# Hybrid trunk on one core: a reordered opening on five PSUM banks, a reordered last head, and the causal mask added by VectorE in seven heads

## The reference

```python
s = jnp.einsum('blhd,bshd->bhls', q_blk, k_all).astype(jnp.float32) * scale
s = s + jnp.moveaxis(fq_blk, 2, 1)[..., None] - f_k[:, :, None, :]
s = jnp.where(key_pos[None, :] <= pos_blk[:, None], s, -jnp.inf)
p = jax.nn.softmax(s, axis=-1).astype(v_all.dtype)
return jnp.einsum('blhs,bshd->blhd', p, v_all)   # indices 'bhls,bshd->blhd' in the original
```

## Time and profile before

| what | value |
|---|---|
| median of 3 runs | 1576.07 us (1575.6 to 1576.43) |
| the profiled execution, its own time | 1575.49 us |
| its span, first to last instruction | 1573.8 us |
| PE busy | 1534.6 us (98%), 9472 matmuls |
| DVE / ACT / POOL busy | 794.0 / 677.1 / 444.7 us |
| granted TensorE clock, mean | 0.999 |

### The profile page before, as it was taken

The page is one execution under the profiler, slowest core; times in us unless marked ns, Lnnn a source line. Parts: engine busy times, 40 slices in busy tenths (PEclk is TensorE's granted clock), DMA queues, the critical chain, the costliest instruction groups (busy, mean ns, idle before and its releaser), DMA issues.

```text
span 1573.8 us, 26349 instructions
## 1 busy us (share of the span) xinstructions
PE 1534.6 (98%) x9472; PEld 1415.8 (90%) x9472; DVE 794.0 (50%) x1751; ACT 677.1 (43%) x1258; POOL 444.7 (28%) x268
## 2 busy tenths in 40 slices
PE   6999999999999999999999999999999999999998
PEld 5999999999999999988888898999999999988776
DVE  5546777676884231436475243444344343435432
ACT  6444443433233322335455344445454545455321
POOL 1214453553221111344343221222222231215000
PEclk9999999999999999999999999999999999999999
DMA  5122223213102111254456536614241423213121
GB/s 154 43 70 61 74 62 101 60 45 86 53 27 57 41 40 40 79 175 160 153 192 145 56 75 53 68 37 74 37 71 44 71 41 63 61 44 141 55 98 70
DMA packets 129510, 121.09 MB, mean 77 GB/s; under 512 B 10290, under 2 KB 113292, under 8 KB 129452
## 3 DMA queue, kind: packets, MB, share of 16 engines
q1 hardware_dynamic: 129452, 120.32, 31.5%
HBM read 101.64 MB, written 18.66 MB: 76 GB/s over the span
## 4 chain that ended last, share of the span: by engine, by line
PE 88%; ACT 4%; DVE 3%; issue 3%; DMA 1%; POOL 1%; SPq 0%; ACTq 0%; DVEq 0%; POOLq 0%
PE PB L759 83%; PE PB L763 5%; DMA XT<-in_x_prompt_dram 1%; ACT L1339 1%; ACT L1804 1%; ACT SB L1893 0%; ACT SQJ L1373 0%; DVE XT L1931 0%; DMA WOR<-in_w_out_odd_dram 0%; DVE SB L1928 0%; ACT WH L1333 0%; POOL WL L626 0%; DMA XS<-in_x_prompt_dram 0%; DVE XS L1928 0%; DVE M L1931 0%
## 5 line engine op out<-in xcount | busy, mean ns | idle before, releaser
L759 PE MATMUL PB<-HH,WH 128*128 128x352 f32 x1872 | 617.5, 330 | 2.5 <-DVE HL L1924 1.6
L759 PE MATMUL PB<-HH,WL 128*128 128x352 f32 x1872 | 601.9, 322 | 0.0
L759 PE MATMUL PB<-HL,WH 128*128 128x352 f32 x1872 | 601.1, 321 | 0.0
L759 PEld LDWEIGHTS PB<-HH,WH 128*128 128x128 f32 x1872 | 351.9, 188 | 17.5 <-issue 10.4
L759 PEld LDWEIGHTS PB<-HL,WH 128*128 128x128 f32 x1872 | 352.9, 189 | 0.2
L759 PEld LDWEIGHTS PB<-HH,WL 128*128 128x128 f32 x1872 | 351.9, 188 | 0.0
L626 POOL TENSOR_TENSOR WL<-WRAW,WH 128x1024 fp32r<-128x1024 f32 x81 | 199.9, 2468 | 534.3 <-ACT WH L1333 527.6
L1333 ACT ACTIVATE WH<-WRAW 128x1024 fp32r<-128x1024 f32 x112 | 118.0, 1054 | 14.3 <-DMA WRAW<-in_w_out_even_dram 6.1
L1893 ACT ACTIVATE SB<-SB,small 128x128 f32<-128x128 f32 (+8 forms) x72 | 53.8, 748 | 78.6 <-DVE small L1928 78.6
L1924 DVE TENSOR_TENSOR Y<-PB,Y 128x128 f32 (+3 forms) x72 | 20.2, 281 | 127.6 <-PE PB L759 127.5
L759 PE MATMUL PB<-PT,VTOK 128*128 128x128 f32 (+2 forms) x624 | 81.5, 274 | 0.0
(11 more groups left out here) (312 smaller groups left out, 2362.6 us busy)
## 6 DMA issues: line engine op xcount, KB each, us to landing
WRAW<-in_w_out_even_dram SPq DMA_DIRECT2D x48, 512.0 KB, 3.6
WRAW<-in_w_in_even_dram SPq DMA_DIRECT2D x44, 512.0 KB, 3.8
WRAW<-in_w_in_odd_dram SPq DMA_DIRECT2D x32, 512.0 KB, 8.2
ACSB<-acs_rows SPq DMA_DIRECT2D x16, 528.0 KB, 5.3
NFB<-nf_rows SPq DMA_DIRECT2D x8, 656.0 KB, 3.9
XS<-in_x_prompt_dram SPq DMA_DIRECT2D x8, 512.0 KB, 6.2
XT<-in_x_prompt_dram SPq DMA_DIRECT2D x8, 512.0 KB, 5.3
x_rows<-OG SPq DMA_DIRECT2D x8, 512.0 KB, 5.4
```

What stands on the lines that cost most here:

```text
L759: return pe.matmul(out, lhsT, rhs, start=start, stop=stop)
```

## The change

- Opening. SP issues the parameter loads after x tile 1, not after tile 2. ACT loads the root's table by a dummy Sqrt before any data is there, and then works tile by tile (square, root). PE turns each of the first three tiles as soon as it is normed, five column blocks into banks 3 to 7, and the parameter rows into bank 2 after tile 0; DEXP is turned later. The first weight tile's chunk 0 is run without turns between, and the turns of group 1 are interleaved with the second weight tile.
- Mask. In heads 0 to 6 the mask matmul is left out; DVE adds `MASKD` to the diagonal 128 columns (PSUM to `SB`), and then runs the bias-and-maximum instruction on them from `SB` to `SB`. The last head keeps the matmul on PE, with one more memset on DVE.
- Last head. `fill` takes a new group bank by bank; ACT's `out_squares` stand ahead of `probs_read`; `YH` of head 6 is copied after the third output weight's high part; POOL's `out_low(5)` goes ahead of `low_of_head(6)`.

```diff
-            if b == 2:
+            if b == 1:
                 for src, (row, n) in (
...
+            if b == 2:
                 load_w(tile_no(W_BC[0], 1, 0), even(XBC0 + 8 * P))
...
         pool.wait_ge(S("n_done"), 16)
+        out_low(5)
         low_of_head(6)
-        for k in range(5, 8):
+        for k in range(6, 8):
             out_low(k)
...
+        for b in range(3):
+            pe.wait_ge(S("xn"), b + 1)
+            for k in range(5):
+                last = turn(PB[x_bank(k)][:, b * P:(b + 1) * P], XS[:, b, k * P:(k + 1) * P])
+                if b == 2:
+                    last.then_inc(S("x_t"), 1)
+            if b == 0:
+                pe.wait_ge(S("rows_in"), 112)
+                turn(PB[2][:, 0:N_ROWS], ROWS[0:N_ROWS, :]).then_inc(S("rows_turn"), 1)
+        for k in range(5, KT):
+            x_turn(0, k)
         for k in range(KT):
-            x_turn(0, k)
+            first_step(W_BC[0], 0, 0, k)
         for k in range(KT):
             if k >= 4:
                 x_turn(1, k - 4)
-            first_step(W_BC[0], 0, 0, k)
+            first_step(W_DT, 0, 7, k)
...
-                mm(PB[3 + i][0:rows, 0:c1 - c0], q, KALL[:, key0 + c0:key0 + c1], stop=c1 < keys)
-
-            mm(PB[3 + i][0:rows, keys - rows - c0:keys - c0], IDENTB[0:rows, 0:rows],
-               MASKD[0:rows, 0:rows], start=False).then_inc(S("sc_mm"), 1)
+                last = mm(PB[3 + i][0:rows, 0:c1 - c0], q, KALL[:, key0 + c0:key0 + c1], stop=not masked or c1 < keys)
+            if masked:
+                last = mm(PB[3 + i][0:rows, keys - rows - c0:keys - c0], IDENTB[0:rows, 0:rows],
+                          MASKD[0:rows, 0:rows], start=False)
+            last.then_inc(S("sc_mm"), 1)
...
+            if g > 0 and filled[g] == 0:
+                for h in banks:
+                    pe.wait_ge(S("f_sq"), h - 2)
+                    pe.wait_ge(S("f_g"), h - 2)
+                    out_odd(h // 2, h % 2, h % 3, list(new))
...
-        x_square(0)
-        x_square(1)
-        x_root(0)
-        x_square(2)
-        x_root(1)
-        x_root(2)
+        act.wait_ge(S("dve_order"), 1)
+        act.activation(SQJ[:, 0:1], ONES[:, 0:1], ACT.Sqrt).then_inc(S("sqrt_set"), 1)
+        act.wait_ge(S("sqrt_set"), 1)
+        for b in range(3):
+            x_square(b)
+            x_root(b)
...
+                if not project and i in (5, 8):
+                    for h in range(i - 5, i - 2):
+                        out_squares(h)
                 if attend and 1 <= i <= NB + 1:
                     probs_read(i - 1)
...
-                    n = (width + 511) // 512
-                    order(dve.memset(MX[0:rows, n:n + 1], -3.0e38))
+                    own = width if not project else width - rows
+                    n = (own + 511) // 512
+                    diagonal = SB[0:rows, own:width]
+                    if project:
+                        order(tt(diagonal, PB[3 + own // 512][0:rows, own % 512:own % 512 + rows],
+                                 MASKD[0:rows, 0:rows], ALU.add))
                     for k in range(n):
...
+                    if project:
+                        order.fence()
+                    order(dve.memset(MX[0:rows, n + 1:n + 2], -3.0e38))
+                    if project:
+                        order(dve.tensor_tensor_reduce(diagonal, diagonal, NFB[0:rows, key0 + own:key0 + width],
+                                                       1.0, -3.0e38, ALU.add, ALU.max, MX[0:rows, n:n + 1]))
+                    else:
+                        order(dve.memset(MX[0:rows, n:n + 1], -3.0e38))
```

More of the change, by code:

```diff
@@ L50, with x_bank @@
 FINAL = (0, 1, 2, 3, 4, 5, SMP, 6, 7)
+def x_bank(i):
+    return X_BANKS[i] if i < KT else RING[(i - KT) % 3]
 def tile_no(first, per, t):
@@ L198, in hybrid_trunk @@
     TOKQ = r("TOKQ", [P, 4, 9, HEADS_B])
+    DEXP = at("DEXP", r.at, [8, 2, HP])
+    DSM = at("DSM", r.at + 512, [8, 2])
     FS = r("FS", [P, 2, P])
@@ L811, in x_turn @@
                 rows = sample_rows(b)
-                last = turn(PB[RING[i % 3]][:, j * P:j * P + rows], XS[0:rows, b, k * P:(k + 1) * P])
+                last = turn(PB[x_bank(i)][:, j * P:j * P + rows], XS[0:rows, b, k * P:(k + 1) * P])
             last.then_inc(S("x_t"), 1)
@@ L848, in _ @@
             first_step(W_DT, 2, 5, k)
+        pe.wait_ge(S("dexp"), 1)
+        turn(PB[3][:, 256:256 + 8], DEXP[:, :, :].rearrange("t j p -> t (j p)")).then_inc(S("rows_turn"), 1)
         w1 = tile_no(W_BC[1], 1, 0)
@@ L1237, in fill @@
             g, n = FILL[i]
[L1238 to L1243, removed]
+            new = range(filled[g], filled[g] + n)
+            banks = range(3 * g, 3 * g + 3)
+            if g > 0 and filled[g] == 0:
[4 more added lines that the diff above has]
+            else:
+                for k in new:
+                    for h in banks:
+                        out_odd(h // 2, h % 2, h % 3, [k])
             filled[g] += n
@@ L1385, in x_high @@
                 act.wait_ge(S("x_t"), i + 1)
-                act.activation(HH[:, k, c0:c0 + n], PB[RING[i % 3]][:, 0:n], ACT.Copy,
+                act.activation(HH[:, k, c0:c0 + n], PB[x_bank(i)][:, 0:n], ACT.Copy,
                                scale=COLS[:, PRE0 + k:PRE0 + k + 1]).then_inc(S("h_hi"), 1)
-        x_square(0)
-        x_square(1)
-        x_root(0)
-        x_square(2)
-        x_root(1)
-        x_root(2)
+        act.wait_ge(S("dve_order"), 1)
[4 more added lines that the diff above has]
+            x_root(b)
         act.wait_ge(S("rows_turn"), 1)
-        order(copy(COLS[:, :], PB[3][:, 0:N_ROWS]))
-        copy(DCOL[:, :], PB[3][:, P:P + 8]).then_inc(S("cols"), 1)
-        order.fence()
+        copy(COLS[:, :], PB[2][:, 0:N_ROWS]).then_inc(S("cols"), 1)
         split_high(tile_no(W_BC[0], 1, 0))
+        act.wait_ge(S("cols"), 1)
+        x_high(0, range(0, 2))
         x_square(3)
-        x_high(0, range(0, 4))
+        x_high(0, range(2, 5))
+        act.wait_ge(S("w_clear"), 1)
+        split_high(tile_no(W_DT, 1, 0))
         x_square(4)
         x_root(3)
-        x_high(0, range(4, 8))
+        x_high(0, range(5, 8))
         x_square(5)
@@ L1885, in turn_steps @@
                     last_head_high(i - 2)
-                if not project and i in (5, 8):
-                    for h in range(i - 5, i - 2):
-                        out_squares(h)
                 if attend and i <= NB:
@@ L1902, in turn_steps @@
                     out_root(2)
-                if attend and project and i == 11:
-                    act.wait_ge(S("y_read"), 9 * t + 9)
-                    copy(YH[:, t, :], Y1[:, t, :]).then_inc(S("y1_hi"), 1)
+                if attend and project and not last and i == 11:
+                    high_of_head(t)
         for b in (6, 7, SMP):
@@ L1910, in _ @@
         act.wait_ge(S("lf_stored"), 32)
-        with order.loop(0, 7, 2) as t:
+        with order.loop(0, 6, 2) as t:
             turn_steps(t)
+        turn_steps(6, last=True)
         turn_steps(7, project=False)
@@ L1970, in _ @@
         x_norm(5)
+        x_low(1, range(0, 2))
         x_mean(6)
-        x_low(1, range(0, 4))
+        x_low(1, range(2, 4))
+        x_norm(6)
         x_mean(7)
-        x_norm(6)
         x_low(1, range(4, 8))
+        x_norm(7)
         x_mean(NB)
-        x_norm(7)
         x_norm(NB)
+        dve.wait_ge(S("rows_in"), 112)
+        dve.tensor_copy(DEXP[:, :, :], DSM[:, :].unsqueeze(2).broadcast_to([8, 2, HP])).then_inc(S("dexp"), 1)
         x_low(2, range(0, 8))
```

65 lines of the change are left out of this document (30 added, 35 removed).

## The result

| kernel | median of the runs | lowest to highest | profiled execution: its time, its span |
|---|---|---|---|
| before, on the same chip | 1575.84 us (4) | | 1575.49, 1573.8 us (its own profile) |
| after | 1559.99 us (4) | 1558.85 to 1561.46 us | 1558.85, 1557.1 us |

The ratio is 0.9896, with a 95% interval of [0.9884, 0.9908]. 1560.0 us had been forecast.

What follows compares the result with a forecast made beforehand. PE was taken as the bound, busy 1534.6 of 1573.8 us. Opening 4.7, mask 6.2 and last head 5.2 sum to 16.1 us: 1559.4 us from the profiled execution, forecast as a 1560.0 us median, range 1555 to 1568.

Steps and rivals of the forecast that it cites:

- Opening: Start of the kernel: reordered loads, table load and turns gain 5.6 us, taken as 4.7; bounds 1 to 7 us.
- Last head: Final head: reordered fill, squares and copies gain 5.2 us, between 2.5 and 6.7.
- the mask costs 0.11 us: Heads 0 to 6: each of 63 mask matmuls costs PE 0.11 us, 6.9 us in all, 6.2 after step 5.
- The term for step 5: Block 5 of seven turns: PE already waits 0.21 us for scaled rows, so removing the mask gains nothing there: -0.8 us.
- DVE's chain: Attention turns: the mask on DVE makes `sm` and `pn` 0.5 to 0.6 us later, hidden from PE, priced at nothing.
- Rival 1: Turns: POOL holds DVE; blocks 0, 2 and 8 miss by 0.2 to 0.4 us, losing 6 us: 1566 us; chance 0.14.
- rival 4: Turns: softmax chain bounds; 1.7 us extra per block loses 2.3 us a turn, 2.2 us loses 42: 1602 us; chance 0.03.
- squares 6 and 7: Opening: sitting between group 1's high parts, they hold PE's last turn about 0.9 us, where the old order lost 0.4.
- DEXP's later turn: Opening: turning DEXP later costs "a bit", part of the step from 5.6 to 4.7 us.
- Rival 2: Opening gives only 1 us, as x tile 2 lands late or PE stays at half pace: 1564 us; chance 0.11.
- bank stalls: Last head, steps 6 and 9: PE's waits for banks go once squares come first, 2.85 and 2.8 us, sum 5.65.
- the memsets: Last head, blocks 1 to 4: two maximum memsets behind the wide instruction cost about 0.1 us each: -0.4 us.

Runs made afterwards that it cites:

- e5_both: The changed kernel with the mask matmul kept on PE in all heads as well, so the mask is added twice; 1564.38 us, ratio 0.9920 to before.
- e7_psum: The changed kernel with one operand of the diagonal bias-and-maximum read from PSUM, leaving the mask out of seven heads; one run, 1561.14 us.
- e6_more: The changed kernel with DVE's mask addition done five times instead of once at the eight prompt blocks of heads 0 to 6; 1571.75 us.
- e1_open: The kernel before with the change to the opening alone; 1570.74 us, ratio 0.9963 to before.
- e8_rows_late: The changed kernel with the seven parameter loads issued after x tile 2, as in the kernel before; 1559.93 us.

## Why the prediction came out right

1. **Sum and mechanism.** 16.1 us were forecast; 1576.07 - 1559.99 = 16.1 us came by the medians, 16.7 us by the spans. The forecast was made against one execution, so 16.7 is the number it should be held to: 0.6 us short, because the opening gave 0.95 us more than its term and the last head 0.25 us more, and the mask 0.5 us less. That the median fell within 0.01 us of 1560.0 us is luck: the four runs lie 2.6 us apart, and 0.4 us of the opening's gain are the two profiles' own.
2. **Mask: 6.2 us forecast, 5.7 us measured.** The step "the mask costs 0.11 us" is the term that was mis-sized. Read from step to step (means of the turns) the saving is 0.07 to 0.14 us, 0.10 on the mean of eight blocks; e5_both, which puts only the matmul back, gives 0.80 us a turn. One place had been read for all 56. The bounds of 0.06 and 0.22 us (the row's duration, which a pipeline overlaps) held, and the right choice was to read starts and not durations. The term for step 5 held: PE's wait went from 0.21 to 0.33 us.
3. **DVE's chain: nothing forecast, nothing measured.** The 0.5 to 0.6 us were too much: from its first instruction to the reduction of the maxima, block 3 took 0.78 us before and takes 1.14 us, block 4 0.98 and 1.27 us, so 0.3 to 0.4 us more. The margin made this error free. Holds came where they were put, at blocks 0, 2 and the sample block 8, and a slight one at block 5 (0.37 us), where ACT's tables hide it. At block 2 the scaled rows were ready 0.26 us ahead of PE. e5_both shows that the chain costs nothing, e7_psum what makes the holds, e6_more that 1.3 us more would have cost 1.7 us a turn. Rival 1's mechanism was there and missed by that 0.26 us; rival 4's price for a delay of 1.7 us, 2.3 us a turn, was too high: e6_more, whose chain is about that much longer than before, lost 1.7 us, and nothing at block 2, where the hold swallowed the delay. Its 42 us, for 2.2 us, no run tests.
4. **Opening: 4.7 us forecast, 5.65 us measured** in the two profiles, 5.3 us by the means of all, 4.9 to 5.4 us in e1_open. Tile 2 was normed at 10.32 (10.5 forecast), the first matmul at 14.53 (15), the first turn of group 1 at 22.55 (22.5). The mis-sized terms are the two taken off at the end: 0.5 us net for squares 6 and 7 between the high parts ("about 0.9 us, where the old order lost 0.4"), and 0.4 us for DEXP's later turn and the rest. Group 1's last turn waited 0.23 us, where the old order waited 0.39 us, and from the first turn of group 1 to its last it took 6.20 us instead of 6.30 us. Without the two the working gives 5.6 us. Rival 2 fell on both counts: tile 2 had landed before ACT asked for it, and the half pace was there, but the low parts were the bound and not PE. That POOL holds the scaling of an x tile ahead of them (1.64 us for 0.75) is in no step of the prediction.
5. **Last head: 5.2 us forecast, 5.45 us measured.** Both bank stalls went, 2.78 and 2.65 us against 2.85 and 2.8 us. In step 3 the wait for WOL turned into one of 1.05 us for SB, whose scaling takes 1.70 us beside POOL, as before: the reordered `out_low(5)` is worth nothing, as forecast. The term that was mis-sized is the 0.4 us taken off for the memsets, which don't show: the two stalls alone are 5.43 of the 5.45 us.
6. **Signs.** PE's work fell by 7.7 us (7 forecast), a turn takes 72.74 us (72.6), XS is waited for 7.5 us (7).

## What to carry to other kernels

Price a small instruction on a full engine by the distance of its neighbours' starts, at several places, and not by its own duration. Before work is put on another engine, read the free time at each step where the full engine needs that chain's result, and of the small work that queues behind the chain. Then look for the one step that has none: there the next gain lies, as the SiLU in step 5 showed. An instruction on VectorE with two inputs in SBUF should be placed away from GpSimd's long ones, or take one input from PSUM. Add up what a trace says of each part at its own place; medians over a few runs don't resolve 1 us in 1560. And read that place in more than one profile: the same opening differed by 0.4 to 0.5 us.

## What the runs showed of the hardware

- An addition with one input in PSUM ran inside GpSimd's instruction at its normal 0.29 us (five in 1.59 us), and an instruction with both in SBUF took 1.39 and 1.70 us and ended 0.14 us after GpSimd's. A scaling with one SBUF input was held too: 1.70 us instead of 0.42 us in step 3 of the last head, 1.64 us instead of 0.75 us in the opening.
- The granted clock was at the 1.2 GHz level behind one wait of 1.7 to 1.9 us in four profiles and not in ten others, for 1.6 us each time. What decides it stays open. In the opening PE ran at that level in some profiles and not in others, and the end of the opening didn't move with it. In the profile of before the matmuls of that stretch show the slow pace while the granted clock is given as 1.00, and in e8_rows_late too (0.29 us apart from 15.62 us on, 1.00 given for 16 to 18 us); the pace of the rows is the surer sign.
